# Last branch of a dilated attention layer: projections in three pieces, scores on quarter tiles, bias and maximum in one instruction

## The chip, the cores and the metric

The kernel runs on one core of a Trainium2 chip. The metric is the time on the device in microseconds (us); smaller is better. The time before is the median of three runs; beside it stands one execution taken by the hardware profiler.

## The reference

One inference step of a small decoder: 1024 prompt tokens and 8 sample tokens (one new token for each of 8 sequences with caches of 256), width 1024. Layer 1 is a gated delta-rule mixer, layer 2 a dilated sliding-window attention, each followed by a squared-ReLU MLP. The attention, which the change touches, is

```
kv = rmsnorm(x, norm_kv) @ w_kv          # 3 branches x (k, v) x 2 kv heads x 64
q  = rmsnorm(x, norm_mix) @ w_q          # 3 branches x 8 heads x 64
for each branch (window, dilation) in (128,1), (512,4), (2048,16):
    s = q . k / 8 - slope_h * distance   # keys at distances 0, d, 2d, .., window
    m = max(s); o = exp(s - m) @ v / sum(exp(s - m)); lse = m + log(sum)
out = sum over branches of softmax(lse) * o, then @ w_o, added to x
```

All inputs and outputs are float32. The keys and values of all branches, for prompt and samples, are outputs too.

## The kernel before

**Products.** Every dense product is done in split precision: a weight w is kept as w_hi and w_lo, an activation as x_hi and x_lo, and one k-step (128 rows of the inner dimension) is three matmuls, hi*hi, hi*lo and lo*hi, into one PSUM bank. The 1032 token columns (1024 prompt, 8 samples) are cut in three at `CUTS` = 0, 352, 704, 1032. Weights arrive by DMA in halves of 512 rows' worth; ScalarE writes w_hi (`split_hi`, L608), VectorE w_lo (`split_lo`, L1118). There are four slots for split units of weights.

**The attention layer** begins with dense products alone: keys and values of branches 2 and 1 and the queries of branch 2. The rest of the dense work, 30 products of 8 k-steps (240 k-steps), is used as filler between the steps of attention: the queries of branch 1, then the queries of branch 0, then keys and values of branch 0, each group with all its tiles in the order of the three column pieces. A loop of 26 steps follows, each with three "places"; `dense_done(place)` says how many k-steps are done at the end of a place: 96 by place 17, then 6 more a place, 240 at place 41 (in step 13). `fill(place)` on TensorE does them, `drain(place)` on VectorE takes finished products one place later (`take`). From place 66 (step 22) on, `fill` does the output projection. Queries go from `q_stage` to memory in HBM and come back as `q_tile`, tile by tile (SyncE: `store_query`, `load_query`, two tiles ahead).

**One step of attention.** Step s works on three tiles of 128 queries. There are 24 tiles: branch 2 (steps 0 to 7), branch 1 (8 to 15), branch 0 (16 to 23). A tile attends to one block of 128 keys (`nk` = 1: all of branch 2, the even tiles of branch 1, the first of branch 0; 13 tiles) or to two (`nk` = 2; 11 tiles). Each tile's 8 heads go in two halves.
- scores (TensorE, L2609): keys lie in `k_mask`, once for each kv head, with the rows of the other head zero, so that one matmul of 128 rows gives the scores of one query pair against both kv heads, 256 * nk columns. Two such matmuls make a half. They go to PSUM banks 3 and 4.
- VectorE adds the bias (`biased`, L1873 for nk = 1 with 512 columns a half, L1879 for nk = 2 with two of 512) and then takes the maximum of four heads at once (`maxima`, L1886).
- ScalarE takes the exponential with the sum of each head (`exps`, L970).
- in the next step TensorE transposes the probabilities (`turn`, L2111), VectorE and ScalarE copy them out (`turned`), and TensorE multiplies by the values (`apply`, L2632, on half-width tiles of 64 output rows).
- ScalarE copies the output (`keep_outputs`, L993), TensorE turns it (`outputs_turn`), VectorE takes it. For branch 0 the three branches are merged (`merge_output`, POOL and ScalarE with it), turned and split for the output projection.

The order on TensorE in step s is written by hand:

```
turn(cur, 0); scores(nxt, 1); outputs_turn; fill(3s); turn(cur, 1)
scores(next, 0); fill(3s + 1); apply(cur); fill(3s + 2)
```

On VectorE it is: biased and maxima of half 0 of nxt, turned(0), drain(3s), biased and maxima of half 1, drain(3s + 1), outputs of the tile before, turned(1), merge work, drain(3s + 2), and in the steps listed in `SPLITS` two weight blocks, which wait for ScalarE's. ScalarE does its part of the split last in a step, behind `keep_outputs`.

**Samples.** The 8 sample tokens have an attention of their own: in step 14 TensorE turns their values (`samples_rows`), VectorE places their queries, SyncE loads constants (old keys and values, bias) into memory that the dense work has left; scores in step 16, shares in 17, the turn in 18, the product with values in 19. In step 14 SyncE also stores branch 0's keys and values (`store_keys(0)`).

Of the kernel before, what the change touches and what calls it, by code (L numbers as in the profile page):

```python
# [24 lines left out]
P = 128  # L25
# [37 lines left out]
          12: ((10, 2, 0),), 13: ((10, 2, 1),), 14: ((11, 3, 0),), 15: ((11, 3, 1),)}  # L63
LOADS = {0: ((6, 0), (6, 1)), 2: ((7, 0),), 3: ((7, 1),), 4: ((8, 0),), 5: ((8, 1),), 8: ((9, 0),), 9: ((9, 1),),
         10: ((10, 0),), 11: ((10, 1),), 13: ((11, 0),), 14: ((11, 1),), 15: ((12, 0),), 16: ((12, 1),),
         }
GROUPS = ((4, (0, 1), 1), (4, (2, 3), 0), (2, (0, 1), 0))
# [7 lines left out]
def dense_done(place):  # L75

    if place < 18:
        return 8 + 88 * (place + 1) // 18 if place >= 0 else 0
    return min(96 + 6 * (place - 17), 240)


def dense_product(n):

    g = n // 12
    return g, GROUPS[g][0], GROUPS[g][1], n - 12 * g

# [85 lines left out]
def build(nc, t):  # L172
# [129 lines left out]
    k_mask = at("k_mask", [P, 2, 2, SEQ], F32, a)  # L302
    v_feat = at("v_feat", [P, 2, SEQ], F32, a)
    q_stage = at("q_stage", [P, 2, CUTS[1]], F32, a)
# [12 lines left out]
    a = [region + KT * NT * 4 + 4 * 2 * SEQ, END]  # L317
    merge = at("merge", [P, 2, 2, 8 * HD], F32, a)
    a = [region + KT * NT * 4 + 4 * (2 * 2 * SEQ + SEQ), END]
    merged = at("merged", [P, 2, 8 * HD], F32, a)  # L320
    out_t = [v_feat[:, n, 0:4 * P] for n in (1, 0)]
# [10 lines left out]
    a = [x_start, x_start + KT * NT * 4]  # L332
    s_keys = at("s_keys", [P, NS, SK], F32, a)
    s_va = at("s_va", [P, NS, P], F32, a)
    s_vb = at("s_vb", [SB, NS, P], F32, a)
    s_bias = at("s_bias", [P, SK], F32, a)
    s_qz = at("s_qz", [P, BRANCH, NS, 32], F32, a)
    s_p = at("s_p", [P, 2, SK], F32, a)
    s_pm = at("s_pm", [P, 2, 2], F32, a)
    s_pt = at("s_pt", [P, 2, 2 * P], F32, a)  # L340
    s_vrow = at("s_vrow", [NS, BRANCH, P], F32, a)
# [13 lines left out]
    def prompt_width(third):  # L355
        return min(CUTS[third + 1], SEQ) - CUTS[third]

    def prompt(third, d=1):

        return slice(CUTS[third] // d, min(CUTS[third + 1], SEQ) // d)  # L360
# [56 lines left out]
    def _(sp):  # L417
# [36 lines left out]
        def store_keys(b):  # L454
            for g in range(2):
                rows = slice(g * HD, (g + 1) * HD)
                sp.dma_start(t["p_k"][rows, b], k_mask[rows, b % 2, g]
                ).then_inc(sem("kv_stored"), L.add("kv_stored", 16))
            sp.dma_start(t["p_v"][:, b], v_feat[:, b % 2]).then_inc(sem("kv_stored"), L.add("kv_stored", 16))

        def store_query(b, n):
            third, tile = divmod(n, 4)
            d = DIL[b]
            sp.wait_ge(sem("product_free"), L.next("product_free"))
            dst = t["q"][:, 4 * b + tile].rearrange("p (r i) -> p r i", r=d)[:, :, prompt(third, d)]
            sp.dma_start(dst, q_stage[:, n % 2, 0:prompt_width(third)].rearrange("p (r i) -> p r i", r=d)
            ).then_inc(sem(f"q{n % 2}_stored"), L.add(f"q{n % 2}_stored", 16))

        def load_query(i):
            b, tile, par, _ = tile_of(i)  # L470
            if tile == 0:
                for n in range(2):
                    sp.wait_ge(sem(f"q{n}_stored"), L.value(f"q{n}_stored"))
# [12 lines left out]
        def attention_traffic():  # L486
# [7 lines left out]
            sp.wait_ge(sem("k_zeroed"), L.next("k_zeroed"))  # L494
# [16 lines left out]
            for step in range(STEPS):  # L511
                for unit, part in LOADS.get(step, ()):
                    weight(U_KVQ + unit, part)
                for place in range(3 * step, 3 * step + 3):
                    for n in range(dense_done(place - 2) // KT, dense_done(place - 1) // KT):
                        g, tiles, _, m = dense_product(n)
                        if tiles == 2:
                            L.skip("product_free")
                        else:
                            store_query(GROUPS[g][2], m)  # L520
                if step + 2 < 24:
                    load_query(step + 2)
                if step == 14:
# [7 lines left out]
                    sp.wait_ge(sem("kv_ready"), L.next("kv_ready"))  # L531
                    store_keys(0)
                if step == 17:
# [65 lines left out]
    def _(act):  # L599
# [335 lines left out]
        def attention_layer():  # L935
# [10 lines left out]
            def keep_values(b, h, bank):  # L946
                act.wait_ge(sem(f"bank{bank}_full"), L.next(f"bank{bank}_full"))
                act.activation(v_keys[:, b % 2, hc(h)], psum[:, bank].rearrange("p (c n) -> p c n", n=P), ACT.Copy
                ).then_inc(sem(f"bank{bank}_free"), L.add(f"bank{bank}_free"))
            for b in (2, 1):  # L950
# [11 lines left out]
            def exps(step, nxt, hs):  # L962
# [4 lines left out]
                skip(*((3, 4) if nk == 2 else (3 + hs,)))  # L967
# [21 lines left out]
            def keep_outputs(step):  # L989
                if step in (1, 17):  # L990
# [9 lines left out]
            for step in range(STEPS):  # L1000
# [5 lines left out]
                if step == 15:  # L1006
                    keep_values(0, 0, 5)
                if step == 17:
# [8 lines left out]
                if step == 15:  # L1017
                    keep_values(0, 1, 5)
                if nxt:
                    exps(step, nxt, 1)  # L1020
                if step == 18:
# [1850 lines left out]
```

## Time and profile before

| | us |
|---|---|
| median of 3 runs | 2722.85 |
| lowest and highest | 2721.39, 2723.74 |
| profiled execution, its own time | 2721.97 |
| span in the profile, first to last instruction | 2720.2 |

TensorE's mean granted clock in the span is 0.991 of full. The profile counts an engine busy from an instruction's start to its (for matmuls modelled) end. The matmuls of one float32 product show as two records. Waits are put down to the instruction whose semaphore came last.

### The profile page before, as it was taken

To read this page: it belongs to the slowest core of one execution; us is meant where nothing else is said; L and a number is where in the kernel's file an instruction comes from. 1 tells how busy PE (TensorE), PEld (TensorE's weight loads), DVE (VectorE), ACT (ScalarE), POOL (GpSimd) and SP (SyncE) were. 2 spreads that over 40 slices of the span, in tenths; PEclk is the share of its full clock that TensorE was granted. 3 is DMA by queue.
4 is the path that set the end of the run, shared out by engine and by line. 5 is a ranking of instruction groups with operands and counts; after the bars stand their busy time and mean duration, and the time that the engine had idled before them with its cause. 6 is when DMAs were issued, how large, how long until landed. Compare 5 with 4: busy or idle time off the path is not lost.

```text
span 2720.2 us, 48302 instructions
## 1 busy us (share of the span) xinstructions
PE 2638.9 (97%) x20476; PEld 2508.2 (92%) x20476; DVE 1553.1 (57%) x2961; ACT 827.6 (30%) x1870; POOL 66.6 (2%) x92
## 2 busy tenths in 40 slices
PE   7999999997899999999999999988999999999998
PEld 6999999996699999999999998864899999999997
DVE  6777777777575444444444736567764444444445
ACT  5444544543141211121112314345531112111211
POOL 0000000000300000000000000002200000000000
PEclk9999999998999999999999999998999999999999
DMA  3111101134311111111111234334111111111111
GB/s 142 48 42 41 41 20 32 34 119 164 106 47 63 47 47 39 56 47 47 40 55 47 97 101 118 96 116 134 59 47 47 47 47 47 47 47 47 47 32 63
DMA packets 81989, 174.32 MB, mean 64 GB/s; under 512 B 21681, under 2 KB 46801, under 8 KB 81060
## 3 DMA queue, kind: packets, MB, share of 16 engines
q1 hardware_dynamic: 73860, 162.72, 18.5%
q10 hardware_dynamic: 7920, 8.56, 1.0%
q8 instruction: 162, 2.65, 0.4%
q14 instruction: 47, 0.39, 0.0%
HBM read 140.28 MB, written 36.21 MB: 65 GB/s over the span
## 4 chain that ended last, share of the span: by engine, by line
PE 89%; DVE 5%; DMA 2%; ACT 1%; issue 1%; POOL 1%; SPq 0%; DVEq 0%; ACTq 0%; POOLq 0%
PE psum L2085 19%; PE psum L2086 19%; PE psum L2087 19%; PE psum L2159 4%; PE psum L2160 4%; PE psum L2161 4%; PE psum L2111 2%; PE psum L2358 2%; PE psum L2609 2%; PE psum L2567 1%; PE psum L2632 1%; PE psum L2568 1%; PE psum L2569 1%; PE psum L2450 1%; DMA x_half<-in_x 1%
## 5 line engine op out<-in xcount | busy, mean ns | idle before, releaser
L2085 PE MATMUL psum<-x_hi,w_hi 128*128 128x352 f32 (+1 forms) x1040 | 334.8, 322 | 0.0
L2086 PE MATMUL psum<-x_lo,w_hi 128*128 128x352 f32 (+1 forms) x1040 | 332.4, 320 | 0.0
L2087 PE MATMUL psum<-x_hi,w_lo 128*128 128x352 f32 (+1 forms) x1040 | 330.9, 318 | 0.0
L1118 DVE SCALAR_TENSOR_TENSOR w_lo<-w_raw,gains,w_hi 128x512 fp32r<-128x512 f32 x380 | 262.1, 746 | 84.7 <-ACT w_hi L608 84.6
L608 ACT ACTIVATE w_hi<-w_raw,gains 128x512 fp32r<-128x512 f32 x380 | 246.9, 712 | 121.5 <-DMA w_raw<-in_w 121.2
L2159 PE MATMUL psum<-x_hi,w_hi 128*128 128x352 f32 (+1 forms) x768 | 273.2, 356 | 1.2 <-DVE pre L1200 1.2
L2085 PE MATMUL psum<-u_hi_b,w_hi 128*128 128x352 f32 (+1 forms) x768 | 247.1, 322 | 0.0
L2085 PE MATMUL psum<-u_hi,w_hi 128*128 128x352 f32 (+1 forms) x768 | 246.7, 321 | 0.0
L2085 PE MATMUL psum<-x_hi_b,w_hi 128*128 128x352 f32 (+1 forms) x768 | 246.6, 321 | 0.0
L2160 PE MATMUL psum<-x_lo,w_hi 128*128 128x352 f32 (+1 forms) x768 | 245.9, 320 | 0.0
L2086 PE MATMUL psum<-x_lo_b,w_hi 128*128 128x352 f32 (+1 forms) x768 | 245.5, 320 | 0.0
L2161 PE MATMUL psum<-x_hi,w_lo 128*128 128x352 f32 (+1 forms) x768 | 245.2, 319 | 0.0
L2087 PE MATMUL psum<-u_hi_b,w_lo 128*128 128x352 f32 (+1 forms) x768 | 245.2, 319 | 0.0
L2087 PE MATMUL psum<-u_hi,w_lo 128*128 128x352 f32 (+1 forms) x768 | 245.2, 319 | 0.0
L2086 PE MATMUL psum<-u_lo_b,w_hi 128*128 128x352 f32 (+1 forms) x768 | 245.0, 319 | 0.0
L2086 PE MATMUL psum<-u_lo,w_hi 128*128 128x352 f32 (+1 forms) x768 | 245.0, 319 | 0.0
L2087 PE MATMUL psum<-x_hi_b,w_lo 128*128 128x352 f32 (+1 forms) x768 | 244.3, 318 | 0.0
L1742 DVE SCALAR_TENSOR_TENSOR relu<-psum,rs 128x352 f32<-128x352 f32 (+1 forms) x192 | 99.1, 516 | 214.2 <-PE psum L2087 206.7
L908 ACT ACTIVATE u_hi_b<-relu 128x352 fp32r<-128x352 f32 (+1 forms) x96 | 47.2, 492 | 519.4 <-DVE relu L1745 519.4
L908 ACT ACTIVATE u_hi<-relu 128x352 fp32r<-128x352 f32 (+1 forms) x96 | 47.2, 492 | 516.8 <-DVE relu L1745 516.8
L2086 PEld LDWEIGHTS psum<-x_lo,w_hi 128*128 128x128 f32 x1040 | 195.5, 188 | 0.5
L2085 PEld LDWEIGHTS psum<-x_hi,w_hi 128*128 128x128 f32 x1040 | 195.4, 188 | 0.5
(373 smaller groups left out, 5542.4 us busy)
## 6 DMA issues: line engine op xcount, KB each, us to landing
w_raw<-in_w SPq DMA_DIRECT2D x190, 512.0 KB, 3.7
q_tile<-scratch_q SPq DMA_DIRECT2D x24, 256.0 KB, 3.0
scratch_att<-o_out ACTq DMA_DIRECT2D x32, 132.0 KB, 2.5
x<-in_x SPq DMA_DIRECT2D x8, 516.0 KB, 9.8
s_state<-in_s_rec_in SPq DMA_DIRECT2D x2, 2048.0 KB, 14.7
out_s_rec<-s_state SPq DMA_DIRECT2D x8, 512.0 KB, 2.6
merge<-scratch_att SPq DMA_DIRECT2D x8, 512.0 KB, 3.7
scratch_o_heads<-head_out ACTq DMA_DIRECT2D x7, 512.0 KB, 2.7
```

Of the source, the lines that this page charges most:

```text
L608: done = act.activation(w_hi[:, slot, 2 * part + k], w_raw[:, part, k], ACT.Copy, scale=gains[:, unit * UW + 2 * part + k:unit * UW + 2 * ...
L908: act.activation(lay.u_hi[:, tile, THIRDS[third]], relu[:, 0:width(third)], ACT.Copy).then_inc(sem("u_hi_ready"), L.add("u_hi_ready"))
L1118: done = v.scalar_tensor_tensor(w_lo[:, slot, 2 * part + k], w_raw[:, part, k], gains[:, unit * UW + 2 * part + k:unit * UW + 2 * part + k ...
L1742: v.scalar_tensor_tensor(r, psum[:, TAKES[n % 6], 0:width(third)], 0.0, rs[:, cols], ALU.max, ALU.mult).then_inc(sem("product_free"), L.ad ...
L2085: mm(out, whi, xh[:, k, cols], start=k == 0, stop=False)
L2086: mm(out, whi, xl[:, k, cols], start=False, stop=False)
L2087: done = mm(out, wlo, xh[:, k, cols], start=False, stop=k == kts - 1)
L2111: done = nc.tensor.transpose(psum[0:cols, bank, at_col:at_col + rows], src, ident[0:rows, 0:rows])
L2159: mm(out, whi, x_hi[:, k, cols], start=k == 0, stop=False)
L2160: mm(out, whi, x_lo[:, k, cols], start=False, stop=False)
L2161: done = mm(out, wlo, x_hi[:, k, cols], start=False, stop=k == KT - 1)
L2358: done = mm(psum[out, bank + r, cols], lhs[rows, c, p], rhs(rows, c, p), start=True, stop=True, tile_position=(r * HD, c * HD))
```

## The change

1. Branch 0's queries, keys and values are cut in pieces of 384, 384 and 264 columns (`LATE_CUTS`) and done in the order of `LATE`: queries of the last piece, queries of the first, keys and values of the last, of the first, then queries and keys and values of the middle piece. `dense_done` spreads them: 96 k-steps at place 17 as before, 192 at place 40, 240 at place 53 (step 17). They use PSUM banks 1 and 2 in turn.
2. Keys are kept once (`k_feat`), not twice with zeros. A half of scores is eight matmuls on 64 x 64 tiles of the array, one for each query pair, kv head and half of the queries, 128 * nk columns each; kv head g goes to bank 3 + g.
3. Bias and maximum are one `tensor_tensor_reduce` a head, which also writes the (negated) scores; ScalarE's exponential starts head by head. Scores of a half wait until the four maxima of the half before are out.
4. On TensorE `scores(nxt, 1)` stands behind `fill(3s)`. The samples' work, now in PSUM bank 0 and in memory of the dense pieces that are done, comes one step earlier from the scores on. The branch-0 values are turned in three parts (steps 15 and 18), its keys and values stored in step 19, and the weight units 10 and 11 are split in steps 17 to 20, not 12 to 15.

```diff
-          12: ((10, 2, 0),), 13: ((10, 2, 1),), 14: ((11, 3, 0),), 15: ((11, 3, 1),)}
+          17: ((10, 2, 0),), 18: ((10, 2, 1),), 19: ((11, 3, 0),), 20: ((11, 3, 1),)}
-GROUPS = ((4, (0, 1), 1), (4, (2, 3), 0), (2, (0, 1), 0))
+LATE = tuple((tiles, third, tile) for tiles, third in ((4, 2), (4, 0), (2, 2), (2, 0), (4, 1), (2, 1)) for tile in range(tiles))
+LATE_CUTS = (0, 384, 768, NT)
...
-    return min(96 + 6 * (place - 17), 240)
+    if place < 41:
+        return 96 + 96 * (place - 17) // 23
+    return min(192 + 48 * (place - 40) // 13, 240)
...
+def dense_bank(n):
+    return n % 3 if n < 12 else 1 + n % 2
...
-                    sp.wait_ge(sem("kv_ready"), L.next("kv_ready"))
+                if step == 19:
+                    sp.wait_ge(sem("kv_ready"), L.next("kv_ready", 2))
                     store_keys(0)
...
-                act.wait_ge(sem("max_ready"), L.next("max_ready"))
                 for n in range(4 * hs, 4 * hs + 4):
-                    act.activation(prob[:, par, n, cols], prob[:, par, n, cols], ACT.Exp,
+                    act.wait_ge(sem("max_ready"), L.next("max_ready"))
+                    act.activation(prob[:, par, n, cols], prob[:, par, n, cols], ACT.Exp, scale=-1.0,
...
-            def maxima(step, nxt, hs):
-                _, _, par, nk = nxt
-                for j in range(2):
-                    v.wait_ge(sem(f"bank{3 + j}_free"), L.value(f"bank{3 + j}_free"))
-                v.tensor_reduce(stats[:, step % 3, 0, hc(hs)], prob[:, par, hc(hs), (2 - nk) * P:2 * P], AXX, ALU.max,
-                                negate=True).then_inc(sem("max_ready"), L.add("max_ready"))
+                cols = slice((2 - nk) * P, 2 * P)
+                v.wait_ge(sem("scores_full"), L.next("scores_full"))
+                for n in range(4 * hs, 4 * hs + 4):
+                    lo = n % 4 // 2 * nk * P
+                    done = v.tensor_tensor_reduce(prob[:, par, n, cols], psum[:, 3 + n % 2, lo:lo + nk * P], bias[:, n, cols],
+                                                  -1.0, -NEG, ALU.add, ALU.min, stats[:, step % 3, 0, n:n + 1])
+                    done.then_inc(sem("max_ready"), L.add("max_ready"))
...
-                keys = k_mask[:, b % 2, :, (tile + 1 - nk) * P:(tile + 1) * P]
+                cols = slice((tile + 1 - nk) * P, (tile + 1) * P)
+                if nxt == tile_of(0) and hs == 0:
+                    for free in ("bank3_free", "bank4_free"):
+                        pe.wait_ge(sem(free), L.next(free)), L.skip(free, -1)
+                else:
+                    pe.wait_ge(sem("max_ready"), L.next("max_ready", 4))
                 for j in (2 * hs, 2 * hs + 1):
...
+                    lo = j % 2 * nk * P
+                    for g in range(2):
+                        rows = slice(g * HD, (g + 1) * HD)
+                        for h in range(2):
+                            part = slice(h * HD, (h + 1) * HD)
+                            done = mm(psum[part, 3 + g, lo:lo + nk * P], q_tile[rows, par, j, part], k_feat[rows, b % 2, cols],
+                                      start=True, stop=True, tile_position=(g * HD, h * HD))
+                done.then_inc(sem("scores_full"), L.add("scores_full"))
...
-                if nxt:
-                    scores(nxt, 1)
                 if step > 1:
                     outputs_turn(step)
                 if step:
                     fill(3 * step)
+                if nxt:
+                    scores(nxt, 1)
```

## Rows read from the trace of the kernel before

**Rows 1.** The page: busy time, share and instructions of each engine over the span.
```profile
PE 2638.9 (97%) x20476; PEld 2508.2 (92%) x20476; DVE 1553.1 (57%) x2961; ACT 827.6 (30%) x1870; POOL 66.6 (2%) x92
```

**Rows 2.** Stretches (start:end, length), busy time of engines, granted clock, DMA share, GB/s.
```profile
1647.50:1692.20 44.70, 44.70 (x276) 39.42 (x275) 29.59 (x52) 20.49 (x76) 0.00 (x0) 1.00 0.44 120
1692.20:1731.50 39.30, 39.11 (x232) 34.09 (x231) 20.14 (x35) 12.69 (x53) 0.00 (x0) 1.00 0.31 88
1731.50:1805.10 73.60, 71.96 (x417) 59.26 (x416) 42.78 (x73) 28.99 (x97) 0.00 (x0) 1.00 0.29 86
1805.10:1829.20 24.10, 18.58 (x95) 12.01 (x94) 16.52 (x33) 13.03 (x42) 0.00 (x0) 0.93 0.53 166
1829.20:1847.20 18.00, 11.90 (x96) 7.54 (x96) 8.62 (x15) 6.66 (x24) 0.00 (x0) 0.81 0.39 118
1847.20:1855.70 8.50, 7.18 (x33) 3.16 (x29) 7.99 (x12) 5.05 (x19) 0.00 (x0) 1.00 0.11 32
1855.70:1901.80 46.10, 39.08 (x188) 22.88 (x189) 34.80 (x65) 25.98 (x89) 18.35 (x36) 0.93 0.50 157
1901.80:1924.50 22.70, 22.70 (x129) 16.52 (x129) 18.64 (x34) 11.80 (x39) 9.01 (x18) 1.00 0.38 119
sum 277.00, PE 255.21 PEld 194.88 DVE 179.07 ACT 124.69 POOL 27.36; mean PE 31.90 PEld 24.36 DVE 22.38 ACT 15.59 POOL 3.42
```

**Rows 3.** Chain of waits in the attention loop: start, length, what, records.
```profile
1640.18 0.44 PE psum L2111 x4
...
1755.73 1.72 PE psum L2609 x4
...
1760.16 1.89 PE psum L2632 x8
...
1762.08 0.60 ACT v_feat L993
1762.68 1.23 ACT w_hi L608 x2
...
1827.33 13.04 DMA q_tile<-scratch_q
...
1844.19 3.11 PE psum L2659 x57
```

**Rows 4.** Groups of VectorE by line, 1632 to 1948: busy, mean ns, idle before.
```profile
L1879 DVE TENSOR_TENSOR prob<-psum,bias 128x512 f32<-128x512 f32 x44 | 28.3, 682 | 0.3
L1886 DVE TENSOR_REDUCE stats<-prob 128x4 f32<-128x1024 f32 x22 | 26.8, 1220 | 2.3
L1118 DVE SCALAR_TENSOR_TENSOR w_lo<-w_raw,gains,w_hi 128x512 fp32r<-128x512 f32 x26 | 18.4, 748 | 41.8 <-ACT w_hi L608 41.8
```

**Rows 5.** Timeline of TensorE in the delta stage: start, length, instruction, records.
```profile
88.59 0.32 PE L2161 MATMUL psum<-x_hi,w_lo 128*128 128x352 f32 x1
88.84 0.69 PE L2358 MATMUL psum<-ident,pair 64*64 64x64 f32 x32
89.36 0.65 PE L2358 MATMUL psum<-pair 64*64 64x64 f32 x32
89.93 0.43 PE L2159 MATMUL psum<-x_hi,w_hi 128*128 128x352 f32 x1
90.20 0.32 PE L2160 MATMUL psum<-x_lo,w_hi 128*128 128x352 f32 x1
90.36 0.32 PE L2161 MATMUL psum<-x_hi,w_lo 128*128 128x352 f32 x1
```

**Rows 6.** Timeline of VectorE in the attention loop.
```profile
1886.01 1.28 DVE L1879 TENSOR_TENSOR prob<-psum,bias 128x512 f32<-128x512 f32 x2
...
1837.90 0.31 DVE L1950 COPY s_keys<-s_kv 128x8 f32<-128x8 f32 x3
```

**Rows 7.** Timeline of TensorE: the samples' last products and what follows them.
```profile
1873.29 0.29 PE L2675 MATMUL psum<-s_pt,s_va 128*128 128x8 f32 x2
...
1876.78 0.64 PE L2111 MATMUL psum<-ident,merged 128*128 128x128 f32 x4
```

More of the change, by code:

```diff
@@ L470, in load_query @@
             b, tile, par, _ = tile_of(i)
-            if tile == 0:
+            if tile == 0 or (b == 0 and tile == 3):
                 for n in range(2):
@@ L1814, in take @@
                 if tiles == 2 and tile == 0:
-                    for g in range(2):
-                        rows = slice(g * HD, (g + 1) * HD)
-                        done = v.tensor_tensor(by_class(k_mask[rows, b % 2, g]), src[rows], scale[rows], ALU.mult)
-                        done.then_inc(sem(mark if g else "dve_order"), L.add(mark if g else "dve_order"))
+                    v.tensor_tensor(by_class(k_feat[:, b % 2]), src, scale, ALU.mult).then_inc(sem(mark), L.add(mark))
                 elif tiles == 2:
@@ L2011, in attention_layer @@
                 if nxt:
-                    biased(nxt, 0)
-                    maxima(step, nxt, 0)
+                    biased(step, nxt, 0)
                 if cur:
@@ L2020, in attention_layer @@
                     samples_queries()
-                if step == 16:
+                if step == 15:
                     samples_keys()
                 if nxt:
-                    biased(nxt, 1)
-                    maxima(step, nxt, 1)
+                    biased(step, nxt, 1)
                 drain(3 * step + 1)
@@ L2539, in attention_layer, with late_values @@
                 stage_begin(n)
+            def late_values(first, last):
+                return [v_feat[:, 0, c * P:(c + 1) * P] for c in range(first, last)]
             def values(b, h):
@@ L2556, in fill @@
                     n, k = divmod(m, KT)
-                    g, tiles, slots, in_group = dense_product(n)
-                    third, tile = divmod(in_group, tiles)
-                    out, cols = psum[:, n % 3, 0:width(third)], THIRDS[third]
-                    if in_group == 0 and k == 0:
+                    _, _, slots, third, tile, cuts = dense_product(n)
+                    cols = slice(cuts[third], cuts[third + 1])
+                    out = psum[:, dense_bank(n), 0:cols.stop - cols.start]
+                    if n in (0, 12, 20) and k == 0:
                         pe.wait_ge(sem("raw_free"), L.next("raw_free", 4))
+                    if n == 12 and k == 0:
+                        L.skip("product_free")
                     if k == 0:
@@ L2702, in attention_layer @@
                 if step == 15:
-                    transposes(5, values(0, 1))
+                    transposes(5, late_values(6, 8))
                 if cur:
                     turn(cur, 1, "q_tile_free")
+                if step == 18:
+                    pe.wait_ge(sem("kv_ready"), L.next("kv_ready"))
+                    transposes(5, late_values(3, 6))
                 if step < 23:
```

184 lines of the change are left out of this document (85 added, 99 removed).

## The prediction, made before the change was run

> **What bounds the kernel now.** I read the page first, for how much of the span TensorE is busy: nearly all [rows 1], so time can come only from its idle or slowed stretches, or from work taken off it. The change lies in the attention layer, so I then cut that layer into stretches at the starts of the products of probabilities and values (`apply`, L2632), one a step; A1 is the apply of step 1, at 1647.5. In that view of stretches [rows 2] the reader is to see three regimes. A1 to A13 (1805.1) is full: 155.8 of 157.6 us busy, clock 1.00. A13 to A17, where the dense work has run out, takes 50.6 us and is busy for 37.7, with the clock at 0.93 of full up to A15 and 0.81 from A15 to A16. A17 to A21 takes 46.1 us for 39.1 busy, clock 0.93, and from A21 on TensorE is full again with the output projection. The chain of waits says what is late in the hole: 13.0 us from issue to landing of one query tile, behind the samples' constants and the stores of keys and values [rows 3]. The groups by line give the prices on VectorE and show its largest wait, 41.8 us for ScalarE's halves of weights [rows 4].
>
> **Prices.** A k-step of the dense work is three matmuls 0.16 us apart [rows 5], so 0.48 us at 352 columns; scaled by columns (estimate) 0.525 at 384 and 0.36 at 264. "Narrow" tiles attend to one block of keys, "wide" ones to two. Four transposes cost 0.44, so a half of turns 0.44 narrow and 0.88 wide, and the turn of outputs 0.44; an apply is 1.89 wide and so about 1.0 narrow, a half of scores 1.72 wide and so 0.86 narrow; ScalarE's copy of an output takes 0.6 and its part of a weight half 1.2 [rows 3], VectorE's 1.4 (two of 0.75 [rows 4]). A tensor_tensor of 512 columns lasts 0.68 us but two take 1.28, so they follow at 0.60; a small operation costs 0.10 (three in 0.31) [rows 6].
>
> **Scores on quarter tiles.** Four matmuls of 64x64 replace what one full-array matmul over zero-padded keys did. If the four run at the same time, each half costs half: 0.43 narrow and 0.86 wide. The trace has such products in the delta stage: 32 records of quarter matmuls between 88.84 and 89.36, 16 products of 64 columns in 0.52 us [rows 5], while one full-array product of 256 columns takes 0.43 (half of 0.86), so 64 columns 0.11, and 16 in a row would take 1.7 us. They do overlap. There are 13 narrow and 11 wide tiles, two halves each: 26 x 0.43 + 22 x 0.86 = 30 us off TensorE. Entering and leaving the group costs: 0.25 in place of 0.16 us from the last dense matmul to the first quarter one, and 0.27 in place of 0.16 behind [rows 5]. The full-array scores have a like seam already, so I charge 0.04 for each of 48 groups, 2 us; by the bare seams it would be 48 x 0.2 = 10. On this the Trainium skill speaks against the change: "TensorEngine Tiling (Array Packing)", Key Properties, says that changing the tiling mode drains the engine. By that rule the seams would be whole costs, and the gaps in the trace agree with it.
>
> **Bias and maximum in one instruction a head.** Before: for a wide half two additions (0.60 each) and a reduction of 1.22 [rows 4, 6]; after: four instructions of 256 columns (128 narrow). The trace shows no such instruction. By columns it is 0.60 - 0.27 = 0.33, since 512 columns more make 0.54 (0.68 to 1.22 [rows 4]); narrow 0.20. That is the low bound. It also has to write out its maximum: one small operation, 0.10, gives 0.43 and 0.30, which I take, as the rows are near. The high bound is no gain by fusing: 0.33 plus a quarter of 1.22, 0.64; narrow about 0.40. The Trainium skill ("VectorE: DVE Perf Modes", the TRN2 errata section) gives a tensor_tensor (N+151)/0.96 ns, 0.42 and 0.29 us; if such instructions did not overlap, against the spacing in the rows, and the write-out came on top, each would be 0.09 dearer and the sum about 12 us worse.
>
> **The new wait.** A half's scores now fill both banks 3 and 4, and the next half's may start only when all four maxima are out. `scores(nxt, 1)` moves behind the first fill, so that between it and `scores(next, 0)` only the second turn is left (0.44 or 0.88). Four instructions take 1.2 narrow, 1.75 wide: TensorE stands 0.8 to 0.9 us in each of 24 steps, with fill, apply and all else queued behind. Before, a fill lay in between.
>
> **Steps 0 to 5, interval by interval.** After (narrow, 14.67 k-steps, 7.1 us): apply 1.0, turns and outputs 1.3, scores 0.94, stand 0.85, seams: 11.3 against 44.7/4 = 11.2 [rows 2], where the old scores cost 1.74. With step 0 I charge 1.2 us lost over five. So the scores' gain is eaten there.
>
> **Dense work spread out.** From place 18 on there were 6 k-steps a place, 18 a step, to place 41; after it are 12.5 a step to place 40 and 11.1 to place 53. The order also starts with 264-column pieces. Intervals, with the same sum:
> A5 to A8: 9.5 + 8.6 + 13.6 = 31.7 against 39.3, gain 7.6. The first is apply 1.0, fills 2.4 + 1.5 + 1.5 (light pieces), turn and outputs 0.9, scores 0.5, until the maxima 1.2, scores 0.5. The last is set by VectorE: it waits for apply, ScalarE's copy and weights (1.0 + 0.6 + 1.2 and gaps, 3.0), splits (1.4), multiplies the new branch's biases (2.4, two as long as the 1024-column reduction), and only then takes maxima (1.2); 8.0 after A7 the scores of half 1 can start (0.5), then VectorE's copy, a take and maxima (0.6 + 0.5 + 1.2), wide scores 0.9, fill 2.2.
> A8 to A13: 11.9 + 11.7 + 12.0 + 10.3 + 12.7 = 58.6 against 73.6, gain 15.0. A typical one is apply 1.0, fill 2.2, turn 0.44, outputs 0.44, fill 2.2, wide scores 0.9, until the maxima 2.1, narrow scores 0.5, fill 2.2.
> A13 to A15: 12.2 + 14.0 = 26.2 against 24.1, since 5.7 us of fill come into each, and the samples' scores (3.1 [rows 3], I take 1.9 at full clock) come one step early: loss 2.1.
> A15 to A16: 10.8 against 18.0. The key and value stores no longer stand before the query tile, its 13 us wait goes and the half clock behind it too: gain 7.2. What is late next is the four maxima again.
> A16 to A17: apply 1.9, fills 5.7, turns and outputs 1.3, scores 0.9 + 0.9, the samples' turn 0.5, stand 1.1: 12.3 against 8.5, loss 3.8.
> A17 to A21: no fill left. Four weight halves moved here from steps 12 to 15. VectorE waits for each (apply 1.9, copy 0.6, weights 1.2, gaps) and has split by 5.3, then maxima 1.8, copy and shares 1.0, maxima 1.8, merge 1.3, copy 0.6: 11.9 a step, and 12.9 in the first, where the samples' last products (3.5 us [rows 7]) precede the second turn. 48.6 against 46.1, loss 2.5.
> A21 to A23: 10.4 + 10.5 against 22.7, gain 1.8: scores of 0.9 in place of 1.7, no splits, one half of scores fewer in the second.
>
> **Hidden.** The k_mask clearing and the second key copy were on VectorE under a full TensorE: nothing. Constants in strided pieces, key stores at step 19, fewer PSUM banks for dense products (two): nothing, while the constants have some 10 us from their issue in step 14 to `samples_keys` in step 15; without that cover it is the rival of the half-filled hole.
>
> **Sum.** -1.2 + 7.6 + 15.0 - 2.1 + 7.2 - 3.8 - 2.5 + 1.8 = 22.0, less 2 for seams: 20 us. The profiled execution took 2721.97 (span 2720.2), 0.9 under the median of the runs shown, 2722.85. 2722 - 20 = 2702.
>
> **Rivals.** Likeliest: the sum above, 2702, its own range 2694 to 2710; chance 0.44.
> Better: the fused instruction is at its low bound, or VectorE's work hides behind turns and fills. Of the 192, the four of the second half count in every step (96) and the other four in some 9 steps: 132 on the path, 72 narrow and 60 wide, at 0.10 less: 13 us, 2689. For it: VectorE is busy for only 179 of the 277 us [rows 2]. Against: on its own path it waits for ScalarE [rows 4]. Chance 0.23.
> Slower: the fused instruction is dear. 20 us are lost at 20/132 = 0.15 us above my price, and by 0.2% (5.4 us) more at 0.19. At the high bound 72 x 0.10 + 60 x 0.21 = 20, so 2722; as custom work it may exceed even that, and 0.25 dearer all through gives 2735. For it: no row shows the instruction, and TensorE now waits on it 24 times. Against: the reduction runs at a column a cycle. Chance 0.13, most of it at 2722 to 2735.
> The hole is only half filled: the samples' constants, loaded in pieces of 128 to 211 columns, hold VectorE at `samples_keys` one step earlier than before, or two dense banks hold TensorE; 6 us at A14 to A16 go, 2708 to 2712. For it: the DMA share up to A15 is already 0.53 [rows 2]. Chance 0.12.
> The seams are whole costs: entering 0.09 and leaving 0.11 for each of the 48 groups [rows 5], 10 us in place of 2: 2710. Against: the old scores paid part of it. Chance 0.05.
> The quarter tiles don't overlap (the change doesn't do what it says): half of 1.72 and 3.44 in place of 0.47 and 0.9 adds 26 x 1.2 + 22 x 2.5 = 86, so 2788. The delta stage speaks against it. Chance 0.03.
>
> **How the numbers follow.** 0.2%, 5.4 us, is about what a measurement tells from no change, so faster means under 2717.4. Faster: 0.44 + 0.23 + 0.12 + 0.05 = 0.84, less 0.04 for cases that meet or a hand sum that errs: 0.80. Same: 0.09. Slower: 0.11, the dear instruction and the 0.03. The range 2688 to 2721 runs from the low bound of the instruction to its high one, and leaves out 0.09 above and 0.08 below.
>
> **What would show it.** The fused instructions should follow at 0.30 and 0.43 us; a half of scores should take under 1 us wide; a wait of scores for maxima of 0.8 us, some 24 times. A15 to A16 should be near 11 us with clock 1.00, A8 to A13 near 59. If intervals A1 to A5 come out over 12 us, or A17 to A21 over 13 each, the instruction or the seam is dearer and the prediction is wrong; if A8 to A13 is under 56, the wait hides.

## The result, and the profile after

The changed kernel takes 2744.38 us (median of 4 runs, 2742.59 to 2744.63), the kernel before on the same chip 2723.30 (4 runs, 2721.39 to 2725.07). The ratio is 1.0074, 95% interval 1.0061 to 1.0086: slower by 20 us, where 20 us faster was forecast. The profiled execution took 2742.59, its span is 2740.8 against 2720.2.

TensorE's line of the page answers to [rows 1]. It has 576 more instructions and is busy for 6.9 us less, yet the span is 20.6 longer: the time went into idle TensorE.

```profile
PE 2632.0 (96%) x21052; PEld 2505.9 (91%) x21052; DVE 1510.5 (55%) x3216; ACT 827.2 (30%) x1871; POOL 66.1 (2%) x92
```

The same stretches as [rows 2], cut at the starts of the same applies (A1, A5, A8, A13, A15, A16, A17, A21, A23), with the same columns:

```profile
1652.50:1698.90 46.40, 44.16 (x372) 36.95 (x371) 26.70 (x106) 20.48 (x76) 0.00 (x0) 1.00 0.42 118
1698.90:1731.40 32.50, 28.79 (x259) 22.58 (x258) 16.98 (x70) 12.68 (x53) 0.00 (x0) 0.95 0.32 89
1731.40:1791.70 60.30, 56.77 (x456) 44.92 (x455) 29.79 (x117) 27.52 (x95) 0.00 (x0) 1.00 0.30 90
1791.70:1838.00 46.30, 29.54 (x250) 23.80 (x249) 12.07 (x53) 10.85 (x39) 0.00 (x0) 0.78 0.26 74
1838.00:1849.40 11.40, 11.28 (x95) 9.08 (x92) 8.32 (x26) 5.76 (x23) 0.00 (x0) 1.00 0.16 42
1849.40:1862.10 12.70, 12.04 (x91) 8.95 (x90) 6.15 (x24) 5.16 (x19) 0.00 (x0) 1.00 0.33 99
1862.10:1921.70 59.60, 42.02 (x296) 28.60 (x296) 32.00 (x112) 30.45 (x92) 17.92 (x36) 0.83 0.50 156
1921.70:1944.70 23.00, 21.55 (x165) 15.94 (x165) 14.51 (x54) 12.68 (x42) 8.97 (x18) 1.00 0.44 143
```

The sum is 292.2 us against 277.0 [rows 2]. Laid beside the forecast (45.7 is 44.7 and four fifths of the 1.2 us charged over five intervals; by the interval of 11.3 it would be 45.2):

| stretch | before | forecast | after |
|---|---|---|---|
| A1 to A5 | 44.7 | 45.7 | 46.4 |
| A5 to A8 | 39.3 | 31.7 | 32.5 |
| A8 to A13 | 73.6 | 58.6 | 60.3 |
| A13 to A15 | 24.1 | 26.2 | **46.3** |
| A15 to A16 | 18.0 | 10.8 | 11.4 |
| A16 to A17 | 8.5 | 12.3 | 12.7 |
| A17 to A21 | 46.1 | 48.6 | **59.6** |
| A21 to A23 | 22.7 | 20.9 | 23.0 |

Two rows miss by 20.1 and 11.0 us, the other six together by 6.3. The stretch ahead of A1 is 4.9 us longer (A1 is at 1652.5, before at 1647.5), in two parts. The first scores start at 1633.77, before at 1632.17; these 1.6 us I don't lean on, since that start lies anywhere from 1632.2 to 1639.6 in the versions of the changed kernel below, all with the same work ahead of it, and from 1631.8 to 1637.8 in three of the kernel before. From the first scores to A1 it is 18.7 us, before 15.4: the second and third half of scores in step 0 each wait 1.2 us for maxima, the rest I can't place. Behind A23 nothing differs by over 0.5.

The chain of waits (start, length, what) goes through the first bad row. The four parts of the samples' constants are issued at 1804.40 to 1806.67, the last lands 20.70 us later, and only then come VectorE's copies, its maxima, and TensorE's scores, which had waited 16.64 us. The granted clock is 0.50 in the 5 us behind that wait (1829.2 to 1834.4), so that matmuls 0.18 us apart before are 0.32 apart and the samples' scores take 3.60 us and not 3.08, as with the clock at 1.00 in the last version below. This answers to the 13.04 us of the query tile in [rows 3].

```profile
1804.40 0.65 SPq L535
...
1806.67 20.70 DMA s_low<-in_s_bias
1827.47 0.24 DVE s_high L1950 x2
1827.71 0.32 DVE prob L1885
...
1829.22 1.13 PE psum L2615 x16
```

SyncE's timeline (start, length, instruction) names the load. The issue of the bias, 105.5 KB, lasts 16.98 us, and it stands behind the third part, `s_vb`: 83 rows of eight pieces of 512 bytes. That this load is the cause is shown by the first experiment.

```profile
1805.80 0.82 SPq L535 DMA_DIRECT2D s_high<-in_s_vb  x1
1806.67 16.98 SPq L535 DMA_DIRECT2D s_low<-in_s_bias  x1
```

The view of transfers from 1812 to 1824 shows what moved meanwhile: one packet of 512 bytes after another, at 21 GB/s and a share of 7.3%, which is 1.2 of the 16 DMA engines. `s_vb` has 83 x 8 = 664 such pieces.

```profile
DMA packets 496, 0.25 MB, mean 21 GB/s; under 512 B 0, under 2 KB 496, under 8 KB 496
q1 hardware_dynamic: 496, 0.25, 7.3%
```

The second bad row holds four steps of 21.6, 12.8, 12.6 and 12.6 us. The chain through the first of them:

```profile
1858.99 4.70 DMA merge_stats<-scratch_att
...
1864.71 0.22 ACT share L1045
...
1866.36 1.33 ACT w_hi L618 x2
1867.71 1.41 DVE w_lo L1133 x2
...
1870.56 1.98 PE psum L2615 x16
1872.54 0.52 PE psum L2681 x2
...
1879.47 2.60 PE psum L2108 x11
1882.07 1.68 PE psum L2615 x16
```

The merge's shares come first on VectorE and ScalarE, when a transfer of 4.70 us has landed; behind them come ScalarE's half of the weights, VectorE's half, the maxima, and TensorE last: it had stood 3.38 us before 1870.56. It stands as long at the same place in the other three steps, 3.46, 3.33 and 3.33 us. In two stretches of the first step the granted clock (third number from the end) goes from 0.95 to 0.51, the lower of its levels (1.2 GHz): behind it scores take 1.98 us where they take 1.0 to 1.1 at full clock, and the samples' last products from 1872.54 to 1879.4, 6.9 us against 3.5 [rows 7].

```profile
1862.10:1870.50 8.40, 4.91 (x29) 3.58 (x28) 3.12 (x13) 3.52 (x9) 1.16 (x6) 0.95 0.40 110
1870.50:1883.70 13.20, 13.14 (x77) 10.52 (x77) 5.71 (x22) 3.28 (x13) 3.69 (x5) 0.51 0.22 76
```

The disputed prices are in the groups by line (busy us, mean ns, idle before) for VectorE and in its timeline in step 16:

```profile
L1885 DVE CUSTOM_DVE_ANT_0 prob<-psum,bias 128x256 f32<-128x256 f32 x88 | 32.0, 420 | 14.7 <-PE psum L2615 14.6
L1885 DVE CUSTOM_DVE_ANT_0 prob<-psum,bias 128x128 f32<-128x128 f32 x96 | 22.1, 287 | 14.9 <-PE psum L2615 14.6 <-DVE v_feat L1832 0.2
L1133 DVE SCALAR_TENSOR_TENSOR w_lo<-w_raw,gains,w_hi 128x512 fp32r<-128x512 f32 x24 | 17.0, 748 | 42.5 <-ACT w_hi L618 42.5
L1885 DVE DVE_READ_ACCUMULATOR2_ANT stats<- 128x1 f32 x184 | 15.3, 83 | 0.0
```

```profile
1850.12 0.42 DVE L1885 CUSTOM_DVE_ANT_0 prob<-psum,bias 128x256 f32<-128x256 f32 x1
1850.47 0.08 DVE L1885 DVE_READ_ACCUMULATOR2_ANT stats<- 128x1 f32 x1
1850.47 0.42 DVE L1885 CUSTOM_DVE_ANT_0 prob<-psum,bias 128x256 f32<-128x256 f32 x1
```

A wide fused instruction starts 0.35 us after the one before it, a narrow one 0.21: the low bound (0.33 and 0.20), not my 0.43 and 0.30. The maximum is written out by an instruction of its own, 83 ns, that starts with the next fused one and so costs nothing between them. The 0.42 and 0.29 us that the formula of the Trainium skill ("VectorE: DVE Perf Modes", the TRN2 errata section) gave are the durations, to the hundredth; the spacing is shorter, as for the tensor_tensor of [rows 6]. Halves of scores take 0.60 narrow and 1.02 to 1.09 wide at full clock (L2615 in the chain, sixteen records each; the 1.13 above is a narrow one at half clock), against 0.47 and 0.9.

### The profile page after: what moved, and what is told of

Its sections match the earlier page's. It is cut to its first block, busy times and chain, and to the rows that moved or that the text cites. A ratio compares the mean times of both kernels' runs of the same rounds, so it can differ in the third digit from the quotient of the medians.

```text
span 2740.8 us, 49662 instructions
## 1 busy us (share of the span) xinstructions
PE 2632.0 (96%) x21052; PEld 2505.9 (91%) x21052; DVE 1510.5 (55%) x3216; ACT 827.2 (30%) x1871; POOL 66.1 (2%) x92
## 3 DMA queue, kind: packets, MB, share of 16 engines
q1 hardware_dynamic: 76233, 162.72, 18.1%
## 4 chain that ended last, share of the span: by engine, by line
PE 88%; DVE 5%; DMA 2%; issue 1%; ACT 1%; POOL 0%; SPq 0%; DVEq 0%; ACTq 0%; POOLq 0%
PE psum L2082 19%; PE psum L2083 19%; PE psum L2084 19%; PE psum L2156 4%; PE psum L2157 4%; PE psum L2158 4%; PE psum L2355 2%; PE psum L2108 2%; PE psum L2615 2%; PE psum L2569 1%; PE psum L2570 1%; PE psum L2571 1%; PE psum L2637 1%; PE psum L2447 1%; DMA x_half<-in_x 1%
```

## The experiments

A ratio compares a version with the kernel before, run beside it. The medians of the kernel before in the three series are 2723.30, 2725.28 and 2723.91 us, so medians of different series are off by up to 2 us. Since the start of the first scores varies by over 7 us from execution to execution, the time from there to A23 in the profiled execution ("the loop" below) says more of an edit in the attention loop:

| version | first scores to A23, us |
|---|---|
| kernel before | 292.3 |
| before, load divided | 291.2 |
| before, ScalarE's halves early | 287.2 |
| before, quarter scores and fused instruction | 295.3 |
| changed kernel | 310.9 |
| changed, old order on TensorE | 317.3 |
| changed, keys and bias first | 299.3 |
| changed, ScalarE's halves early | 294.2 |
| changed, load divided | 299.1 |
| divided, samples' products later | 297.1 |
| divided, fill in step 0 | 296.4 |
| divided, halves early | 280.3 |
| all together | 279.2 |
| all together, keys and bias first | 276.9 |

The first is the load by itself. `s_vb` is loaded in two parts, everything else as in the changed kernel.

```diff
-for dst, name in (..., (s_vb, "s_vb"), ...):
+for dst, src in (..., (s_vb[0:80], t["s_vb"][0:80]), (s_vb[80:SB], t["s_vb"][80:SB]), ...):
```

> The changed kernel, but the samples' constant s_vb (83 rows) is loaded by two transfers, rows 0 to 79 and rows 80 to 82; same pieces of 512 bytes, same step. In the changed kernel the transfers run at 350 GB/s until 1810 and then at 21 GB/s to 1827, and VectorE waits 18.8 us in step 15. Theory 1 (83 rows can't be dealt out over the 16 DMA engines, so one engine carries all 664 pieces): the constants land within 8 us, the wait of 18.8 us falls under 2, the kernel takes 2744 - 17 = 2727 us. Theory 2 (the strided pieces as such are slow, whoever carries them): landing stays at 20 us, 2744. Theory 3 (the constants land early but TensorE then waits for maxima or weights): the wait falls, but less than 10 us come back, above 2734.

Measured: 2732.21 (2728.02 to 2736.65), ratio 1.0027, interval 1.0016 to 1.0037. SyncE's timeline and the chain of waits: both parts are issued within 2.79 us, and the bias lands 5.66 us after its issue.

```profile
1813.06 2.79 SPq L536 DMA_DIRECT2D s_high<-in_s_vb  x2
1815.90 0.81 SPq L536 DMA_DIRECT2D s_low<-in_s_bias  x1
```

```profile
1815.90 5.66 DMA s_low<-in_s_bias
```

A13 to A15 falls from 46.3 to 33.3, the run by 12 us. VectorE's wait for the constants is still 5.7 us. Theory 1 holds, with a rest: the strided pieces are the same and are fast, so they weren't it. That the number of rows decides, and not the mere cut in two, is supported by the share of one engine above; another cut of the 83 rows was not run.

**The same load in the kernel before.**

> The kernel before, but s_vb is loaded as rows 0 to 79 and rows 80 to 82. Theory 1 (its 83 rows sit on one DMA engine there too and hold up the query tile behind them, which took 13 us to land): the tile lands in about 4 us, the half-clock stretch from 1836 to 1848 shrinks, 2723 - 7 = 2716 us. Theory 2 (the tile waits behind the stores of keys and values and the number of transfers, not behind one engine): within 2 us of 2723.

Measured: 2723.85 (2718.93 to 2725.97), ratio 0.9994 (0.9984 to 1.0005). In SyncE's timeline the second issue behind `s_vb`, a small store, falls from 7.60 to 0.44 us (first line before, second line this run), and the longest landing of a query tile from 13.0 to 7.8; the time stays.

```profile
1814.56 7.60 SPq L528 DMA_DIRECT2D out_s_kv_new<-s_kv  x1
1814.91 0.44 SPq L529 DMA_DIRECT2D out_s_kv_new<-s_kv  x1
```

The slow load was in the kernel before too, in whole rows of 4 KB. There it cost 1 us in the trace of the loop and nothing that the time shows, with ScalarE's halves as late as they were; the same kernel with early halves, further down, puts the query tile behind it on TensorE's path.

**Keys and bias first, the load undivided.** VectorE waits for these two only.

```diff
+for dst, src, mark in ((s_keys[:], t["s_keys"], "attention_constants_landed"), (s_bias[:], t["s_bias"], "attention_constants_landed"),
+                       (s_va[:], t["s_va"], "s_values_landed"), (s_vb[:], t["s_vb"], "s_values_landed")):
+    sp.dma_start(dst, src).then_inc(sem(mark), L.add(mark, 16))
```

> The changed kernel, where the samples' keys and bias are loaded first and the keys' copies on VectorE wait for these two alone; the values (s_vb undivided, 83 rows) have a semaphore of their own and are needed two steps later. Theory 1: the 20 us of the hole are VectorE's wait alone, and nobody needs the values so early: near the version with the divided load (2732) or up to 5 better, 2727 to 2732, with VectorE's wait for constants under 6 us. Theory 2: the slow rows hold the queue or one DMA engine, so that the next query tiles come late: 2738 or more, with a wait of scores for a query tile in place of VectorE's.

Measured: 2730.92 (2724.93 to 2734.60), ratio 1.0019 (1.0008 to 1.0030). The time is what theory 1 gives and the mechanism is half theory 2's. A13 to A15 is 27.8, VectorE's wait 2.6; but A15 to A16 is 17.0 where it was 11.4. In SyncE's timeline the next issue (the first line) inherits the wait, 18.60 us, and the query tile behind it starts only at 1830.71; in the chain TensorE's scores wait for it.

```profile
1811.29 18.60 SPq L538 DMA_DIRECT2D out_s_kv_new<-s_kv  x1
...
1830.71 0.42 SPq L484 DMA_DIRECT2D q_tile<-scratch_q  x1
```

```profile
1830.71 3.80 DMA q_tile<-scratch_q
```

**The order on TensorE.** `scores(nxt, 1)` goes back ahead of the outputs' turn and the first fill, as before the change.

```diff
+                if nxt:
+                    scores(nxt, 1)
                 if step > 1:
                     outputs_turn(step)
                 if step:
                     fill(3 * step)
-                if nxt:
-                    scores(nxt, 1)
```

> The changed kernel with scores(nxt, 1) put back ahead of outputs_turn and fill(3s), as in the kernel before; nothing else. Theory 1 (the stand of TensorE at scores, 0.8 to 1.2 us a step, comes from the order, since only a turn lies between two halves of scores): the waits of scores for maxima, 43 us in 22 cases of which 16.6 are the constants', fall by 10 us or more, 2744 - 12 = 2732 us. Theory 2 (VectorE is late anyway, and the first half's maxima then become what scores(nxt, 1) waits for): the wait moves from one half to the other, within 4 us of 2744.

Measured: 2748.08 (2745.69 to 2754.22), ratio 1.0088 (1.0065 to 1.0112). TensorE waits 48.3 us for maxima where it waited 40.5. Theory 1 falls. The interval overlaps that of the changed kernel (1.0061 to 1.0086), so the time alone doesn't tell them apart; the loop is 6.4 us longer in the trace, with 2.7 us more in A1 to A5 and 4.0 more in A8 to A13, which speaks for the new place of the scores.

**Scores and fused instruction alone, in the kernel before.** Quarter tiles, one copy of the keys and `tensor_tensor_reduce`, in the old order and with the old dense pieces.

```diff
-                v.tensor_reduce(stats[:, step % 3, 0, hc(hs)], prob[:, par, hc(hs), (2 - nk) * P:2 * P], AXX, ALU.max, negate=True)
+                for n in range(4 * hs, 4 * hs + 4):
+                    done = v.tensor_tensor_reduce(prob[:, par, n, cols], psum[:, 3 + n % 2, lo:lo + nk * P], bias[:, n, cols],
+                                                  -1.0, -NEG, ALU.add, ALU.min, stats[:, step % 3, 0, n:n + 1])
...
+                    pe.wait_ge(sem("max_ready"), L.next("max_ready", 4))
```

> The kernel before with the quarter-tile scores on unmasked keys and the fused bias and maximum (both halves' order on TensorE as before, dense work in its old place, the samples' work and the weight splits as before). Theory 1 (scores and fused maxima are a gain by themselves; the changed kernel lost by the constants' transfer and by the moved work): 2723 - 10 = 2713 us, with half-scores of 0.65 and 1.05 us and the fused instructions 0.21 and 0.34 us apart. Theory 2 (one wait for all four maxima costs as much as the quarter tiles save): 2723, within 3 us. Theory 3 (seams and waits cost more): over 2728.

Measured: 2726.03 (2724.10 to 2732.12), ratio 1.0009 (0.9999 to 1.0019), no gain. Where the cheaper scores went: first TensorE's waits (total, times, longest), then the stretch A5 to A8.

```profile
PE psum L2597 <- DVE stats L1869: 31.6, 17, 5.8
```

```profile
1698.40:1742.40 44.00, 40.80 (x304) 35.04 (x303) 17.80 (x67) 12.69 (x53) 0.00 (x0) 0.92 0.27 77
```

44.0 us against 39.3 [rows 2], at 0.92 of the clock, and A1 to A5 is 49.1 against 44.7; from A8 to A21 8.0 us are won. Against the 30 us that the forecast took off TensorE stand 31.6 us of waits for maxima. The kernel before waited 9.1 us at the same place:

```profile
PE psum L2609 <- DVE prob L1879: 7.6, 6, 2.9
PE psum L2609 <- DVE prob L1873: 1.5, 1, 1.5
```

So 22.5 us of waits are new. With the 6.7 us by which the halves of scores are dearer than forecast (below) that is 29 of the 30. The split between the two is worked out and not tried: the run changes scores and fused instruction together.

**ScalarE's part of the weights earlier.** With the divided load, the block that writes `w_hi` stands behind the first exponentials of a step, no longer last in it.

```diff
                 if nxt:
                     exps(step, nxt, 0)
+                if step in (7, 17, 19):
+                    act.wait_ge(sem("product_free"), ...)
+                for unit, slot, half in SPLITS.get(step, ()):
+                    split_hi(U_KVQ + unit, slot, (half,))
```

> As the run with the divided transfer of s_vb (2732 us), and ScalarE's weight halves (split_hi) stand behind the exponentials of half 0 of their step, not at its end behind apply's copy; VectorE's halves stay at the end. Theory 1 (the loss from A17 to A21, 59.5 us against 46.1 before, comes from VectorE waiting for those halves, 3.6 us and more in each of four steps, now that the splits stand there, with no fill on TensorE to cover it): A17 to A21 falls to about 50, A7 to A11 gains a few us, the wait of VectorE for ScalarE's halves (42.7 us) falls under 10, 2732 - 14 = 2718 us. Theory 2 (it comes from the samples' last products at half clock and from the merge's transfers): the wait falls, but A17 to A21 stays over 57 and the time within 4 us of 2732.

Measured: 2712.05 (2708.34 to 2715.69), ratio 0.9947 (0.9928 to 0.9967), 20 us under the divided load alone. A7 to A8 goes from 14.1 to 10.0, A17 to A21 from 59.5 to 43.9, its first step from 21.4 to 15.3, while A21 to A23 gives back 1.5; the first stretch below is A17 to A18, the second A18 to A21.

```profile
1847.10:1862.40 15.30, 14.67 (x106) 11.15 (x105) 9.63 (x35) 6.92 (x21) 5.71 (x11) 0.81 0.44 130
1862.40:1891.00 28.60, 21.58 (x198) 12.93 (x195) 22.13 (x79) 21.75 (x71) 14.58 (x25) 0.98 0.77 240
```

TensorE's stand in the first step is gone with it. The clock falls there all the same, in the middle of the samples' last products, with TensorE busy all through:

```profile
1853.60:1856.30 2.70, 2.70 (x28) 2.70 (x25) 2.31 (x10) 2.01 (x6) 2.21 (x2) 1.00 0.15 56
1856.30:1858.00 1.70, 1.70 (x11) 1.70 (x11) 0.45 (x1) 0.00 (x0) 0.00 (x0) 0.58 0.00 0
```

**The same move with the undivided load, and in the kernel before.**

> The changed kernel with its undivided load, and only ScalarE's parts of the weight halves moved ahead, behind the first exponentials of a step. Theory 1: the weights' wait and the load's are separate losses and add up: 2744 less 20, 2724, with A17 to A21 near 44 and A13 to A15 still 46. Theory 2: what is won ahead of the hole waits in it for the same load, so that only A17 to A21 gains: 2728 to 2732.

Measured: 2725.11 (2720.76 to 2733.45), ratio 1.0007 (0.9997 to 1.0016). A17 to A21 is 44.0, A13 to A15 still 45.9. The divided load gave 12 us, the early halves give 19, both together 32, and in the loop 11.8, 16.7 and 30.6: two losses that add up.

> The kernel before with the same move of ScalarE's parts of the weight halves. Its VectorE waits 41.8 us for them, but under a TensorE that has dense work. Theory 1: the wait costs only where no fill covers it: no change, 2720 to 2726, with VectorE's wait gone. Theory 2: it cost the kernel before as well: under 2717.

Measured: 2721.83 (2717.84 to 2724.47), ratio 0.9989 (0.9980 to 0.9999). VectorE's 41.8 us of waiting for ScalarE [rows 4] are gone from its waits, and that is worth about 2 us (0.3 to 5.4 by the interval), where the same move is worth 19 in the changed kernel. But it is not nothing in the trace: A8 to A15 takes 90.4 us and not 97.6, and 3.8 of the 7.2 are lost again in A15 to A16, 21.9 for 18.1. There TensorE waits 8.7 us for the query tile, which is issued behind the slow load and the stores (first its landing, then the wait: total, times, longest):

```profile
1827.90 14.40 DMA q_tile<-scratch_q
PE psum L2609 <- DMA q_tile<-scratch_q: 8.7, 1, 8.7
```

That points to two losses one behind the other in the kernel before, each hiding part of the gain of mending the other; it is not shown, since early halves and divided load together were not run there.

**The samples' last products later in step 18**, behind the next scores, where the turn doesn't wait for them (with the divided load).

> As the run with the divided transfer, and the samples' last products (32 small products, 6.9 us at half clock between 1872 and 1879 in the changed kernel) stand in step 18 behind scores(next, 0), not ahead of turn(cur, 1). Theory 1 (they hold up the second turn and through it VectorE's copy and the apply): A17 to A18 falls from 21.4 to 17 or less and about 4 us come back, 2728. Theory 2 (the stand in that step is VectorE's and the merge's): within 1 us, the products only move.

Measured: 2727.70 (2726.00 to 2730.38), ratio 1.0011 (1.0001 to 1.0020), against 2732.21 without, measured at another time. The first step of A17 to A21 falls from 21.4 to 18.8 us, the second rises from 12.8 to 14.5: the clock is 0.77 and then 0.70 where it was 0.68 and then 0.87, the slow stretch moved on with the products. That is 0.9 us in the trace, which is theory 2. The medians differ by 4.5. Of the profiled executions, this one is 2.0 us shorter from the first scores to A23 and 7.3 ahead of them, where the edit doesn't reach, so I don't count the difference of the medians as the edit's.

**A fill between the scores of step 0** (with the divided load).

> As the run with the divided transfer, and in step 0 fill(1) stands between scores(0, half 1) and scores(1, half 0), where otherwise three halves of scores follow each other with only their maxima between them. Expected by theory 1 (each half must wait 1.1 us for the four maxima): 1 to 1.5 us come back ahead of A1, nothing else moves, 2731. By the rival (the query tile's landing sets that stretch): nothing.

Measured: 2730.92 (2725.27 to 2733.82), ratio 1.0017 (1.0008 to 1.0027). By the time inconclusive: 1.3 us under the divided load alone, with intervals that overlap. In the trace it is 17.7 us from the first scores to A1, against 18.7 to 19.8 in the four versions with the same order there, which speaks for theory 1.

**All together**, and then all together with keys and bias first.

> The divided transfer, ScalarE's halves behind the exponentials of half 0, the samples' last products behind scores(next, 0), and fill(1) between the scores in step 0, together. Theory 1 (each of them is a loss of its own on TensorE's path): 2732 - 14 - 4 - 1 = 2713 us, under the kernel before. Theory 2 (VectorE's and the merge's chain sets A17 to A21 whatever TensorE does): 2725 or more.

Measured: 2709.65 (2706.00 to 2715.23), ratio 0.9941 (0.9920 to 0.9963). The time is theory 1's, but it is not told apart from that of the early halves with the divided load (0.9947), so the last two edits are not shown to add anything. In the trace 3.8 us come back ahead of A1, and A17 to A21 loses 4.4.

> All mends together (divided load, ScalarE's halves early, the samples' last products later, a fill in step 0) and the samples' keys and bias loaded first with a wait of their own. Theory 1: the wait for constants that is left in the divided version, 5.7 us, goes: 2704 to 2707. Theory 2: it hides behind the next wait of the same step: 2709 to 2711, as without it.

Measured: 2707.79 (2705.05 to 2711.92), ratio 0.9940 (0.9923 to 0.9956), some 16 us faster than the kernel before. VectorE's wait for constants falls from 5.7 us in the divided version to 1.9, and the hole is short and at full clock (A13 to A15):

```profile
1787.20:1814.90 27.70, 26.70 (x250) 21.42 (x249) 12.18 (x53) 10.73 (x39) 0.00 (x0) 1.00 0.46 123
```

A13 to A15 was 32.1 with all but this last edit. The two medians differ by 1.9 us, less than their runs spread, so between its two theories the time doesn't decide, though the stretch speaks for the first. Both versions place the samples' products late; A17 to A21 is 48.7 and 48.3 in them and 43.9 with the early halves alone. The version without that edit was not run.

## Why the prediction was wrong

**The step that failed** is in "Hidden": constants in strided pieces were put at nothing (the term of A13 to A15 was -2.1 and measured -22.2), since they "have some 10 us from their issue in step 14 to `samples_keys` in step 15". They needed 23, from 1804.40 to 1827.4. The rival of the half-filled hole named the place and the waiter, VectorE at `samples_keys`, but gave 6 us and a chance of 0.12. The hole took 20.1 more than forecast, and with nobody waiting for the load (keys first) it takes 27.8, within 1.6 of the forecast 26.2. Of these, 1.2 are the samples' scores: I had taken 1.9 us for them at full clock and read the 3.1 of [rows 3] as slowed, but the clock was 1.00 there (1844.2 to 1847.2), and they take 3.08 in the last version, at full clock too. What I lacked was the rate. The size of the pieces I had seen; that 83 rows go through one engine I had not asked. The Trainium skill has the rule, in "DMA: Bandwidth & Descriptors", under "Why a DMA increments its semaphore by 16 and not by 1": a DMA from SP's queue uses the largest number of engines up to 16 that divides the slowest dimension on both sides. By that rule 83, a prime, gives one engine and 80 gives 16. The trace agrees: 7.3% of 16 engines and 21 GB/s for the 83 rows, 5.66 us for what stood behind the 80 and the 3. And a row of before had hinted at it, had I read it: the second issue behind `s_vb` lasted 7.60 us there.

**The second step** is the term of A17 to A21, -2.5, which measured -13.5. Its mechanism was right: apply, copy, weights, split, maxima in series, 11.9 a step forecast and 12.7 found in the last three. Mis-sized was the first step, 21.6 for 12.9, and what the sum had no term for is, first, the shares of the merge ahead of ScalarE's half, which put the split's end at 1869.12, 7.0 us after the apply's start and not 5.3. Second, the clock at 0.51 for the 13.2 us behind, in which the samples' products take 3.4 us more than at full speed, the scores 1.0 and 0.7 and the turns some 1.3 more. Together that is 8.1 of the 8.7 us. What lowered the clock stays open: TensorE had stood 3.38 us just before, but the clock falls in this step with the halves early too, where TensorE was busy for 7.3 of the 7.9 us before, and in the kernel before it stayed at 1.00 through the same products (1873.3 to 1876.8). That ScalarE's place in its order made the stretch long is shown: moved ahead, it takes 43.9. In the kernel before the move brings only about 2 us; in its trace 2.8 are won from A1 to A13, where TensorE was full, and of 4.8 won from A13 to A15 the wait for the query tile takes back 3.8. I had read the 41.8 us as a weakness of one rival, and had left ScalarE last in its step in every interval. The sign that I had named, over 13 us each from A17 to A21, came true in the mean (14.9), but not for the reason given with it: the instruction was not dearer.

**Right, by the rows.** A5 to A8 gained 6.8 (7.6), A8 to A13 13.3 (15.0), A15 to A16 6.6 (7.2, though not for the stores alone: 5.2 of the query tile's 13.0 us went with the divided load), A16 to A17 lost 4.2 (3.8), A1 to A5 1.7 (about 1). The better rival's condition came true, the fused instruction at its low bound; its 13 us did not: intervals A1 to A13 came out 3.2 us over the forecast, not under it. The quarter scores cost 0.13 and 0.1 to 0.2 us a half more than forecast, 26 x 0.13 + 22 x 0.15 = 6.7 us, which ate half of that (worked out, not tried by itself). The stand at the scores was forecast as 0.8 us some 24 times; leaving out the one for the constants it is 23.9 us in 18 cases: 0.56 in the steps up to A7, 1.1 in three further ones and 3.3 to 3.5 in each step from A17 to A21. That a wait for maxima would eat the scores' gain was the forecast for steps 0 to 5, and quarter scores with the fused instruction in the kernel before, 3.0 us longer in the loop, bear it out for the whole. A21 to A23 was 2.1 worse than forecast; the cause stays open. So does part of the 3.3 us from the first scores to A1, and what the seams cost by themselves. The quarter tiles overlap.

## What to carry to other kernels

Price a load by its rows and their layout, not by its bytes: ask how many engines its row count can use, and who issues behind it on the same queue. A wait that costs little under a full engine can cost much more once the filler work is spread away from it, here 19 us for 2: when work is moved out of a stretch, reprice every wait in the stretch where it lands, and put what others wait for first in its engine's order. When mending one loss brings little, look for a second one just behind it before calling the first harmless. Work taken off the bounding engine is a gain only where its next input is already there.

## What the runs showed of the hardware

A load of 332 KB in 83 rows ran at 21 GB/s on about one of 16 DMA engines, and the next issue on SyncE's queue took 16.98 us, the one behind it in the other order 18.60; in rows of 4 KB the second issue behind it took 7.60, and with the rows cut 80 and 3 that behind both 0.81. The read of the accumulator (83 ns) starts with the next fused instruction and adds nothing to the spacing of 0.35 us (256 columns) and 0.21 (128). TensorE's granted clock was 0.51 in the 13.2 us after a stand of 3.38 us in a stretch of little use (busy for 4.9 of 8.4 us), although TensorE was busy for 13.1 of those 13.2. Like stands of 3.46, 3.33 and 3.33 us in the next three steps were followed by stretches at 0.74, 0.72 and 1.00. In the version with early halves the clock fell from 1.00 to 0.58 with no such stand before it, while products of 8 columns ran one after another; before the change it stayed at 1.00 through the same products.
